# Weight splits by halves in turn, and the first part's roots behind ten tiles, around four norms

## The reference

```
for l in range(2):
    hc = rmsnorm(ctx) * (1 + csc1) + csh1          # layer 1 needs only keys and values of it
    hx = rmsnorm(x) * (1 + sc1) + sh1
    y  = token_mixers(h @ w_in[l])                 # retention, Fourier mixing, short convolution
    x  = x + g1 * (y @ w_out[l])
    x  = x + g2 * conv_ffn(rmsnorm(x) * (1 + sc2) + sh2, ffn_w_up[l], ffn_conv_w[l], ffn_w_down[l])
    # in layer 0 the context stream goes through the same two lines
return rmsnorm(x, final_norm_g)
# rmsnorm(x) = x * rsqrt(mean(x * x) + 1e-6) over the 1024 features
```

## Time and profile before

| | us |
|---|---|
| median of 3 runs | 1538.02 (1535.97 to 1538.82) |
| the profiled execution | 1536.42 |
| its span, first to last instruction | 1534.6 |
| TensorE busy | 1507.7 (98%) |
| VectorE busy | 982.7 (64%) |
| GpSimd busy | 927.7 (60%) |
| ScalarE busy | 325.7 (21%) |

### The profile page before, as it was taken

One profiled execution on the slowest core, in us unless ns is written; L12 is line 12 of the kernel. 1 busy time (PEld: TensorE's weight loads), 2 busy tenths in 40 slices (PEclk: granted clock), 3 DMA queues, 4 the chain that ended last, 5 costly groups with the idle time before them and its releaser, 6 DMA issues.

```text
span 1534.6 us, 23340 instructions
## 1 busy us (share of the span) xinstructions
PE 1507.7 (98%) x8932; PEld 1360.0 (89%) x8932; DVE 982.7 (64%) x1434; ACT 325.7 (21%) x518; POOL 927.7 (60%) x844
## 2 busy tenths in 40 slices
PE   7999999999999999999999999999999999999997
PEld 5899998998999999999999989877788888888886
DVE  4899565788777957779566888468646431431444
ACT  3502112314222002210122124111414210210221
POOL 2566333666555655548555657665577776777773
PEclk9999999999999999999999999999999999999999
DMA  9445111442223432235222433232232222223222
GB/s 387 167 155 169 42 56 35 142 150 80 95 86 124 151 124 91 100 110 203 85 73 92 158 115 120 90 97 69 68 98 83 96 96 96 96 96 110 96 94 98
DMA packets 50086, 172.25 MB, mean 112 GB/s; under 512 B 6240, under 2 KB 8800, under 8 KB 48992
## 3 DMA queue, kind: packets, MB, share of 16 engines
q1 hardware_dynamic: 47616, 167.27, 32.1%
q10 hardware_dynamic: 2400, 4.05, 0.9%
HBM read 165.00 MB, written 2.10 MB: 109 GB/s over the span
## 4 chain that ended last, share of the span: by engine, by line
PE 89%; DVE 6%; ACT 2%; DMA 1%; issue 1%; POOL 1%; SPq 0%; DVEq 0%; ACTq 0%; POOLq 0%
PE pair L1494 76%; PE pair L1627 4%; PE aux L1796 3%; DVE aux L928 2%; PE pair L1796 1%; DMA start_slot<-in_start_mods 1%; PE aux L1868 1%; PE aux L1893 1%; PE aux L1907 1%; ACT h_hi L708 1%; PE aux L1572 1%; PE aux L1913 1%; DVE h_lo L1329 1%; DVE x L1388 0%; PE aux L1960 0%
## 5 line engine op out<-in xcount | busy, mean ns | idle before, releaser
L589 POOL TENSOR_SCALAR w_hi<-raw 128x512 fp32r<-128x512 f32 (+1 forms) x410 | 309.1, 754 | 534.0 <-PE pair L1494 447.5
L591 POOL TENSOR_TENSOR w_lo<-raw,w_hi 128x512 fp32r<-128x512 f32 (+1 forms) x410 | 602.2, 1469 | 34.4
L1494 PE MATMUL pair<-h_hi,w_hi 128*128 128x384 f32 (+1 forms) x1620 | 487.8, 356 | 3.8 <-ACT h_hi L672 1.2
L1494 PE MATMUL pair<-h_lo,w_hi 128*128 128x384 f32 (+1 forms) x1620 | 481.2, 352 | 1.1 <-DVE h_lo L1329 0.7
L1494 PE MATMUL pair<-h_hi,w_lo 128*128 128x384 f32 (+1 forms) x1620 | 480.4, 352 | 0.0
L1494 PEld LDWEIGHTS pair<-h_hi,w_hi 128*128 128x128 f32 x1620 | 293.0, 188 | 33.6 <-issue 5.3
L1494 PEld LDWEIGHTS pair<-h_lo,w_hi 128*128 128x128 f32 x1620 | 295.7, 188 | 23.5 <-DVE h_lo L1329 1.6
L1494 PEld LDWEIGHTS pair<-h_hi,w_lo 128*128 128x128 f32 x1620 | 296.3, 188 | 19.1
L928 DVE CUSTOM_DVE_ANT_0 aux<-mod_slot,c_b 128x1024 f32<-128x1024 f32 x120 | 185.9, 1549 | 2.1
L1430 DVE SCALAR_TENSOR_TENSOR tg<-pair,vecs,tg 128x255 f32<-128x255 f32 (+2 forms) x174 | 96.4, 554 | 104.5 <-ACT tg L901 97.5
L1494 PE MATMUL pair<-hid_hi,w_hi 128*128 128x384 f32 (+1 forms) x486 | 147.5, 358 | 0.1
(11 more groups left out here) (218 smaller groups left out, 1497.8 us busy)
## 6 DMA issues: line engine op xcount, KB each, us to landing
raw<-in_slabs SPq DMA_DIRECT2D x204, 512.0 KB, 3.5
mod_slot<-in_mods SPq DMA_DIRECT2D x80, 512.0 KB, 4.0
start_slot<-in_start_mods SPq DMA_DIRECT2D x8, 1024.0 KB, 16.8
x<-in_x SPq DMA_DIRECT2D x4, 768.0 KB, 8.1
out<-fin SPq DMA_DIRECT2D x16, 128.0 KB, 1.9
rot<-kT ACTq DMA_DIRECT2D x16, 64.0 KB, 2.4
rot<-Y ACTq DMA_DIRECT2D x16, 64.0 KB, 3.3
rot<-kT SPq DMA_DIRECT2D x16, 64.0 KB, 2.3
```

Source lines behind the costliest of these rows:

```text
L589: nc.gpsimd.tensor_scalar(w_hi[p][:, a:b], raw[p][:, a:b], 1.0, 1.0, ALU.mult, ALU.mult).then_inc(split, 1)
L591: nc.gpsimd.tensor_tensor(w_lo[p][:, a:b], raw[p][:, a:b], w_hi[p][:, a:b].bitcast(fp32), ALU.subtract).then_inc(split, 3 if narrow(s) else 1)
L1494: ins = nc.tensor.matmul(out[:, place:place + b - a], wt, xt[:, a:b], start=first and k == 0, stop=last and k == 2)
```

## The change

TensorE runs part 1 of the last two slabs in turns: four tiles of the even slab, four of the odd, the rest of the even, the rest of the odd. The sums of part 0 go behind five of these tiles (`SUMS_AT`), its roots behind ten (`ROOTS_AT`). ScalarE takes part 0's root ahead of the even slab's square of part 1. VectorE inverts it ahead of the wait for the even slab, and adds that slab's square behind the scales of blocks 0 and 1 (behind block 0's output in D). GpSimd splits the next two slabs as even first half, odd first half, even second half, odd second half, for A, B and C; `split_ready` gives the values of `split` to all who wait on it.

```diff
--- before.py
+++ after.py
@@ -106,6 +106,16 @@
     return PLAN[0, "dft"] + NLF <= s < PLAN[0, "dft"] + NLF + NCC
 
 
+def split_ready(s, half):
+
+    firsts = [PLAN[0, "up", 0], PLAN[1, "kvq"], PLAN[1, "up", 0]]
+    if type(s) is int and s in firsts:
+        return 4 * s + 2 + 4 * half
+    if type(s) is int and s - 1 in firsts:
+        return 4 * s + 4 * half
+    return 4 * s + 2 + 2 * half
+
+
 def pair_uses(s):
 
     return (s - sum(dft_slabs(l) for l in range(DEPTH) if PLAN[l, "dft"] < s)) // 2
@@ -134,6 +144,7 @@
 HIGH_LAG, LOW_LAG = 1, 6
 SUMS_BEHIND, ROOTS_BEHIND = (0, 3), (0, 7)
 NT = 5
+SUMS_AT, ROOTS_AT = 5, 10
 
 
 def pool_lows_before(name, part, k):
@@ -525,7 +536,7 @@
                         m += MODS_FIRST_OUT[i + 1] // 2
 
             for s in range(PLAN[0, "up", 0] + 2, PLAN[1, "kvq"] + 2):
-                sp.wait_ge(split, 4 * (s - 1))
+                sp.wait_ge(split, split_ready(s - 2, 1))
                 load_slab(s, s % 2)
                 load_mods(m, MODS_AT.get(s - 2, 0))
                 m += MODS_AT.get(s - 2, 0)
@@ -558,7 +569,12 @@
                 sp.wait_ge(split, 4 * (s - 1))
                 load_slab(s, 1)
                 s += 1
-            load_slabs(s, (PLAN["end"] - s) // 2)
+            up = PLAN[1, "up", 0]
+            load_slabs(s, (up + 2 - s) // 2)
+            for s in (up + 2, up + 3):
+                sp.wait_ge(split, split_ready(s - 2, 1))
+                load_slab(s, s % 2)
+            load_slabs(up + 4, (PLAN["end"] - up - 4) // 2)
             for part, (_, a, b) in enumerate(norm_parts("final")):
                 for k in range(KB):
                     sp.wait_ge(out_ready, KB * part + k + 1)
@@ -587,7 +603,7 @@
                 elif n:
                     pool.wait_ge(done, s - 1)
                 nc.gpsimd.tensor_scalar(w_hi[p][:, a:b], raw[p][:, a:b], 1.0, 1.0, ALU.mult, ALU.mult).then_inc(split, 1)
-                pool.wait_ge(split, 4 * s + 2 * half + 1)
+                pool.wait_ge(split, split_ready(s, half) - 1)
                 nc.gpsimd.tensor_tensor(w_lo[p][:, a:b], raw[p][:, a:b], w_hi[p][:, a:b].bitcast(fp32),
                                         ALU.subtract).then_inc(split, 3 if narrow(s) else 1)
 
@@ -604,8 +620,13 @@
             for s in range(PLAN["end"]):
                 if s in behind:
                     lows(behind[s])
-                for half in range(2):
-                    split_half(s, half)
+                if s + 2 in behind:
+                    for half in range(2):
+                        for p in range(2):
+                            split_half(s + p, half)
+                elif s + 1 not in behind:
+                    for half in range(2):
+                        split_half(s, half)
 
         @block.scalar
         def _(act):
@@ -716,9 +737,9 @@
                 for k in (KB - 2, KB - 1):
                     act.wait_ge(part_added, at_ + k - (KB - 3))
                     square(k, 0, mid)
+                root(0)
                 act.wait_ge(*drained_by(first + KB - 2))
                 square(KB - 2, mid, ncol)
-                root(0)
                 if sh is not None:
                     high(0, 0)
                     high(0, 1)
@@ -1099,15 +1120,17 @@
                 add_part(KB - 2, 0, KB - 1)
                 if mods_in is not None:
                     mods_in()
+                invert(0)
                 dve.wait_ge(done, first + KB - 1)
                 update(KB - 2, 1, drained[0])
-                add_part(KB - 2, 1, KB + 1)
-                invert(0)
                 if sc is None:
                     finish(0, 0)
+                    add_part(KB - 2, 1, KB + 1)
                 else:
-                    for k in range(3):
-                        scale(0, k)
+                    scale(0, 0)
+                    scale(0, 1)
+                    add_part(KB - 2, 1, KB + 1)
+                    scale(0, 2)
                 dve.wait_ge(done, first + KB)
                 update(KB - 1, 1, drained[1])
                 if sc is None:
@@ -1497,7 +1520,7 @@
 
             def begin(p, s, uses):
 
-                pe.wait_ge(split, 4 * s + 2)
+                pe.wait_ge(split, split_ready(s, 0))
                 if uses is not None:
                     pe.wait_ge(drained[p], uses)
 
@@ -1615,7 +1638,7 @@
                 _, a, b = norm_parts(name)[part]
                 opens = n == 0 and (part == 0 or a == T)
                 if part == 0 and n == 4 and 0 in halves_:
-                    pe.wait_ge(split, 4 * s + 4)
+                    pe.wait_ge(split, split_ready(s, 1))
                 hi_ready, lo_ready = ready(part, n) if ready is not None else (None, None)
                 if hi_ready is not None and 0 in halves_:
                     pe.wait_ge(*hi_ready)
@@ -1681,16 +1704,16 @@
                     for n in range(len(order)):
                         ins = part_tile(p, s0 + p, n, *one, 0, None)
                     ins.then_inc(part_done, 1)
-                for p in range(2):
-                    pe.wait_ge(part_added, at_ + p + 1)
-                    for n in range(len(order)):
-                        if p and n == 4:
-                            part_roots(name, 0)
-                        part_tile(p, s0 + p, n, *one, 1, None)
-                    if p == 0:
+                for i, (p, n) in enumerate([(p, n) for a, b in ((0, 4), (4, len(order))) for p in range(2) for n in range(a, b)]):
+                    if i in (0, 4):
+                        pe.wait_ge(part_added, at_ + p + 1)
+                    if i == SUMS_AT:
                         for w in free:
                             pe.wait_ge(*w)
                         part_sums(name, 0)
+                    elif i == ROOTS_AT:
+                        part_roots(name, 0)
+                    part_tile(p, s0 + p, n, *one, 1, None)
                 if name == "final":
                     part_sums(name, 1)
                     part_roots(name, 1)
```

## The result

| | median, us | executions | against before |
|---|---|---|---|
| before | 1537.26 (1535.86 to 1539.49) | 19 | |
| after | 1539.90 (1538.79 to 1542.09) | 19 | 1.002, 95% interval 1.0014 to 1.0027 |

The account below looks back on a forecast made before the run. TensorE, busy 1507.7 of 1534.6 us, waits around the norms for VectorE's chain up to the last update. That update's delays at four norms sum to +2.85 us on the median of 1538.02, giving 1540.9; range 1537.4 to 1543.0.

Parts of the forecast that it names:

- step 1: Ahead of the first part's roots at the four norms: TensorE's wait goes, worth 1.32 us in all.
- step 2: Tiles in turns: the even slab's VectorE update comes 2.81 us later at two norms, 2.55 at the other two.
- step 3: VectorE behind three norms: scale 0 follows the even slab's update by 0.40 us, which alone shifts it +0.26, -0.12 and +0.39.
- step 4: VectorE's add between scales falls into GpSimd's w_lo at three norms, costing 0.52, 0.84 and 1.13 us in place of 0.40.
- step 5: VectorE's last update at the four norms moves by +0.78, +0.72, +1.13 and +0.22 us, in sum +2.85.
- step 6: GpSimd's halves in turns: the odd first half, some 2 us earlier, gains nothing; the even second half loses nothing.
- GpSimd first: Rival: at w_lo's end the queued w_hi beats the add at three norms, +2.1, together +4.95 us, 1543.0; chance 0.15.
- TensorE's pace: Rival: the h_hi chain has slack, so the 1.32 us from the roots' wait is kept, 1536.7; chance 0.08.
- free add: Rival: GpSimd's halves land elsewhere, so the add costs 0.40 us three times, +1.56, 1539.6; chance 0.22.

Follow-up runs that it names:

- scales_first: The after kernel with scales 0 and 1 ahead of the even slab's update on VectorE, the add behind scale 2: 1537.01 us, 1.0008 against before.
- slab_order: The after kernel with GpSimd's halves slab by slab again, tiles still in turns: 1542.25 us, 1.0031 against before.
- splits_wait: The after kernel with GpSimd's third half held until the add of the even slab's squares is done: 1539.56 us, 1.0014 against before.
- chain_only: The after kernel with tiles and halves slab by slab, the rest of the change kept: 1534.57 us, 0.9989 against before; measured again, 1535.04 us, 0.9988.
- add_last: The after kernel with the even slab's add moved behind the last update on VectorE: 1538.49 us, 1.0013 against before.
- turns_only: The after kernel with sums, roots, ScalarE's and VectorE's order put back, only tiles and halves in turns: 1547.10 us, 1.0073 against before.
- chain_add_last: The chain_only kernel with the even slab's add moved behind the last update on VectorE: 1536.60 us, 0.9998 against before.

## Why the prediction held, point by point

**Sums, roots, root (step 1).** Right. The roots' wait is gone from the waits' view, and in A TensorE leaves its tiles 6.93 us behind the anchor (354.61) in place of 7.29 (354.24 less 346.95). It gained nothing by that: it waited 0.80 for block 0 where it had waited 0.25.

**The turns (step 2).** Right. The even slab's update was put at 5.75, 5.37, 5.43 and 5.04 us behind the anchors (352.70 less 346.95 and so on); it came at 5.69, 5.31, 5.43 and 5.06.

**VectorE's order (step 3).** Right: scale 0 is 0.40, 0.41 and 0.40 behind that update, and scales_first shows that this is where the time goes.

**The add beside GpSimd (step 4).** Its three costs were 0.52, 0.84 and 1.13; from the add's start to the next scale's it was 0.52 (355.09 to 355.61), 0.85 and 1.08 (1156.67 to 1157.75). The rule of the Trainium skill (SBUF — State Buffer, Who interferes with whom), that the two lock each other out for a whole instruction, agrees with the add of 1.16 and the w_hi of 0.79 behind it.

**The sum (step 5).** Forecast for the last updates +0.78, +0.72, +1.13 and +0.22, measured +0.72, +0.67, +1.06 and +0.22. Together 2.85 forecast, 2.67 in the stretches, 2.64 by the medians. The median itself came out 1.0 below the forecast because the median of before over more executions is 1537.26, not 1538.02, and for 0.2 of the sum. Two things in the sum were not clean. For D I took 0.36 us from the add to the last update, where step 3 says 0.40; the measured +0.22 fits the 0.36. And the sum has no term for TensorE's granted clock: the executions of after with 0.998 have a median of 1539.59, 2.3 us above before, and those with a lower clock raise the median by 0.3. That so much of the sum came out is the mechanism; that the clock's part stayed that small was luck.

**The halves (step 6).** Nothing gained, nothing lost, against before: the stretches of after leave no room for more, though no run has the halves in turns alone. But I had weighed the halves in turns against before alone, and there their early odd half is of no use. With the tiles in turns it is: slab_order lost more, about 1 us at a clock of 0.998 and 2.2 in its profile, since the odd slab's first half then stands behind the even slab's late second half in GpSimd's queue. In that profile the clock fell behind TensorE's stall in A, and did not behind those in B and C.

**The rivals.** GpSimd first did not happen: each add was served ahead of the next w_hi, which was stretched to 0.79 or 0.80. TensorE's pace is out: it left early and waited. The free add was mispriced: I took the add's 1.3 us to come off the time if it were free, and splits_wait freed it for 0.3. What I had left out there is that a split moved away from the add meets the h_lo; in A and B there was room for it, in C not. No run frees the add and leaves the splits where they were, so what a free add alone would be worth is not shown.

What stays open: why A to B lost 0.80 where the last update moved by 0.72, and B to C 0.61 for 0.67; the differences are at the size of what repeats (chain_only and chain_only_2 differ by 0.14 in A to B).

## What to carry to other kernels

Work that is moved earlier gains only if its consumer's queue lets it through: here the roots came early, but the in-order VectorE queue held the scale behind an update that the same change made late. Before interleaving two accumulations, ask who waits for the first one to be complete. The rest of the change, without the turns, was worth 1.4 to 1.6 us: a change that bundles several moves can hide a gain in one of them. And a side engine that streams through the critical stretch (GpSimd's splits) sets by its own phase what a VectorE instruction with two inputs in SBUF costs: the add took 0.41 us with no split beside it, 1.16 beside a w_lo in after, 1.52 in add_last.

## What the runs showed of the hardware that I had not expected

The granted clock of TensorE. In turns_only a wait of 2.84 us was followed by 0.50 for 4 us and 0.65 for 4 more, waits of 2.05 and 1.95 by 0.60 and 0.50, and one of 2.42 in A by no fall; in slab_order, where TensorE was busy for 1.67 of the 3 us from 355 to 358, the next 3 us had 0.60, while behind the wait of 1.83 in C it stayed at 1.00. So the length of the wait alone does not tell whether the clock falls. In the profile of after, the waits of 0.80 and 1.01 us left the clock at 1.00 in the stretches around A, B and C. But the 19 executions of after spread with it: the seven with a mean granted clock of 0.998 took 1538.79 to 1539.90 us, the five with 0.997 took 1539.24 to 1540.64, the seven with 0.995 or 0.996 took 1540.61 to 1542.09. The change has gathered idle time of TensorE in one place, and it may be that some executions pay for that in clock; of the 33 executions of the three kernels without the turns (chain_only, chain_only_2, chain_add_last) none shows less than 0.997, but neither do the 11 of splits_wait, which has the turns. Where the others lose it is not shown, as the one profile of after is of an execution with 0.998.
